# Three token tiles of an expert layer: V rows gathered per pick, or a whole V table multiplied by scattered weights

## The chip, the cores and the metric

The kernel runs on one core of one Trainium2 chip. The metric is device time in microseconds of one execution. The kernel before takes 4022.99 us (median of three runs, 4022.44 to 4024.96).

## The reference, cut to what matters

The reference is one block of an encoder over 1,024 tokens of width 1,024: a combined projection, an SSD mixer, neighbourhood attention, a merge and an output projection with a residual add, and then a layer of many small experts (PEER), a residual add and a last RMS norm. The change touches the expert layer, of which this is the core:

```python
PEER_HEADS = 8; PEER_NKEYS = 128; PEER_EXPERTS = 128 * 128; PEER_TOPK = 16; PEER_CHUNK = 128
def chunk(xc):                                   # 128 tokens
    q = (xc @ w_q).reshape(PEER_CHUNK, PEER_HEADS, 2, PEER_DHALF)
    s = jnp.einsum('thzd,znd->thzn', q, sub_keys).astype(jnp.float32)
    s1, i1 = lax.top_k(s[:, :, 0], PEER_TOPK)
    s2, i2 = lax.top_k(s[:, :, 1], PEER_TOPK)
    ...                                          # the 16 best pairs of each head: top, eidx
    gate = jax.nn.softmax(top, axis=-1)
    act = jax.nn.gelu(jnp.einsum('thkd,td->thk', u[eidx], xc).astype(jnp.float32), approximate=False)
    return jnp.einsum('thk,thkd->td', (gate * act).astype(v.dtype), v[eidx])
# then h = h + g2 * peer(n2), out = rms_norm(h, final_g)
```

Each token picks 8 x 16 = 128 experts. Tables u and v have 16,384 rows of 1,024 f32 (4 KB a row, 67.1 MB a table). The output of a token is the sum of its 128 picked v rows, each with its weight (gate times GELU of the dot product of the token with the picked u row).

## The kernel before

The kernel is written engine by engine, with semaphores. A front half (`stage_condition`, `stage_front`, `stage_ssd`) makes the projections and part of the SSD mixer. `stage_tail` does the rest. Its time is divided into slots. A tile has 128 tokens, and there are 8 tiles (TT = 8). Slot n = 128 i + j belongs to pick j of tile i, and each engine goes through all slots in order and does in a slot what is listed for it there:

- POOL issues the gather of U rows for pick j (L2459): an indirect DMA that brings, for each of the 128 tokens, the u row that it picked, 128 rows of 4 KB into one of RU = 6 places of a ring. It first waits until the place was used (`u_used`).
- DVE forms the 128 dot products of a U gather with the tokens' rows, which lie in PSUM (L2637), and from slot to slot also the routing (top 16, best pairs) of the tile that comes next.
- A grain is two heads, 32 picks. When its dot products are done, ACT takes GELU (L2489) and DVE multiplies by the gates (`weigh`, L2586). PE transposes the grain's indices and weights (`turn_index`, `turn_weight`), and ACT spreads the weights into a matrix (L2500).
- POOL gathers the V rows of the grain (L2452): 32 indirect DMAs, each with 32 picks of four tokens, into one of RV = 12 places. A V gather comes 45 slots behind its pick, one in a slot. PE multiplies every four of them by the spread weights and adds them up in PSUM (`add_experts`, L2683); after the fourth grain of a tile, DVE adds the residual and norms, and SP stores the tile.
- Between these, in the same slots, run the "lane" jobs: for the six later tiles gates, late SSD, attention, merge, output projection and query scores (L1775 are the products of 128x128 weights with 512 columns, f32). They are placed in slots by a cost table, pass by pass, so that the tiles 2p and 2p+1 are ready 12 slots before slot 256 p. The last lane job lies ahead of tile 6: tiles 6 and 7 have none.

So in every slot POOL issues one U gather and, from slot 45 on, one V gather: 1,024 of each, 512 KB each. All loads and stores that are not indirect go through SP's one queue, in program order.

In `stage_front`, SP first loads the blocks w_x of the x projection and copies weights for later from one place in memory to another (`kept_scr`, L487); then it goes through `items`, the gate projections: eight blocks n of 512 columns, each times 8 or 2 token tiles. For block n+1 it loads two halves of w_z (`load_z`, L465) and stores each result (`v_scr`, `zg_scr`, L505) from one of four staging places:

```python
for m, (n, t) in enumerate(items):
    if n + 1 < CB and t in (0, 1):
        sp.wait_ge(z_lo, n * KD + (t + 1) * KH)
        load_z(2 * (n + 1) + t)
```

Of the kernel before, what the change touches and what calls it, by code (L numbers as in the profile page):

```python
# [19 lines left out]
P = 128  # L20
SEQ, DM = 1024, 1024
# [27 lines left out]
LATE_BLOCKS = 6 + 2 + 2 + QW // HALF  # L49


def build_program(nc, a, out):
# [20 lines left out]
    mask_scr = scratch("mask_scr", [P, 4, P])  # L73
    late_ssd = (x_scr, state_scr, bc_scr, tab_scr, mask_scr)
# [3 lines left out]
    with top:  # L78
# [29 lines left out]
        with mid:  # L108
# [12 lines left out]
            with front:  # L121
# [8 lines left out]
                stage_front(nc, a, opener, banks, sem, w_in, ident, ones, n1, cT, X, BT, CT, dt, dA, rpb_scr, zg_scr, v_scr, qk_scr, mod_scr, rpm_scr, kept_scr,  # L130
# [4 lines left out]
        stage_tail(nc, a, opener, banks, sem, ident, mod_scr, rpm_scr, n1_scr, qk_scr, zg_scr, v_scr, y_scr, h_scr, w_scr, kept_scr, w_in,  # L135
# [213 lines left out]
def stage_front(nc, a, opener, banks, sem, w_in, ident, ones, n1, cT, X, BT, CT, dt, dA, rpb_scr, zg_scr, v_scr, qk_scr, mod_scr, rpm_scr, kept_scr, ahead, ps_x0, x_order, split_room, rows_kept):  # L349
# [22 lines left out]
    with ctx:  # L372
# [22 lines left out]
        with ExitStack() as room:  # L395
# [11 lines left out]
            b_ada = sb("b_adaB", [MB, P])  # L407

# [20 lines left out]
        s_kept_w = sem("b_keptw")  # L429
        s_bias, s_kept = [sem("q_bias0"), sem("q_bias1")], [sem("q_kept0"), sem("q_kept1")]  # L430
# [25 lines left out]
        with nc.Block() as block:  # L456
            @block.sync
            def _(sp):
# [29 lines left out]

                for m, (n, t) in enumerate(items):
# [33 lines left out]
                sp.wait_ge(s_kept_w, 16 * LATE_BLOCKS)  # L523

            @block.gpsimd
            def _(pool):
                nc.gpsimd.memset(padded[:, :, 0:2], 0.0).then_inc(edge_done, 1)
# [646 lines left out]
def stage_tail(nc, a, opener, banks, sem, ident, mod_scr, rpm_scr, n1_scr, qk_scr, zg_scr, v_scr, y_scr, h_scr, w_scr, kept_scr, w_in, y_rstd, late_ssd, y_kept, out, s_out):  # L1174
# [14 lines left out]
    with ctx:  # L1189
# [8 lines left out]
        h = n2  # L1198
        qs = sb("qs", [P, 2, QW])
        small = qs[:, 1, :]  # L1200
        ring = sb("ring", [P, (RU + RV) * DM])
        u_rows = ring[:, 0:RU * DM].rearrange("p (r d) -> p r d", d=DM)
        v_rows = ring[:, RU * DM:].rearrange("p (r d) -> p r d", d=DM)
# [21 lines left out]
        idx_f = sb("idx_f", [P, RI, PICKS])  # L1225
# [3 lines left out]
        weight = sb("weight", [P, PICKS])  # L1229
# [12 lines left out]
        lstat = sb("lstat", [P, 4])  # L1242
        nmax = sb("nmax", [P, 2])
        rsum = sb("rsum", [P, 4])
        rinv = sb("rinv", [P, 4])
        ystat = sb("ystat", [P, 2])
# [38 lines left out]
            sem("f_accread"), sem("f_fmean"), sem("f_froot"), sem("f_fin"), sem("f_chain"))  # L1285

# [945 lines left out]
        with nc.Block() as block:  # L2232
# [26 lines left out]
            def _(pool):  # L2259
                nc.gpsimd.iota(iota_i[:, :], pattern=[[1, TOPK]], base=0, channel_multiplier=0).then_inc(iota_done, 1)  # L2260
                nc.gpsimd.memset(spread[:, :, :], 0.0).then_inc(zero_done, 1)
# [461 lines left out]
```

## Time and profile before

| | |
|---|---|
| median of three runs | 4022.99 us (4022.44 to 4024.96) |
| span of the profiled execution | 4023.9 us, from the first to the last instruction |
| PE, DVE, POOL, ACT busy | 69%, 61%, 53%, 21% of the span |
| moved by DMA | 1,423 MB, 354 GB/s over the span |
| of it by POOL's queue (indirect DMAs and a few more) | 1,086.75 MB |
| of it by SP's queue | 332.95 MB |

The three runs lie on both sides of the span of the profiled execution. POOL's busy time holds the generation of its DMAs, not their transfer. The front half ends at about 900 us, where the first U gather is issued; the slots of `stage_tail` fill the rest. L2474 copies the normalized rows of a tile into PSUM at the tile's first slot, when the last dot product of the tile before is done; its eight starts, 897.7, 1283.3, 1706.4, 2102.9, 2517.6, 2885.9, 3287.9 and 3620.4 us, cut the tail into tiles.

### The profile page before, as it was taken

What the parts mean: (1) busy time and instruction counts of PE and PEld (TensorE: products, weight loads), DVE (VectorE), ACT (ScalarE), POOL (GpSimd) and SP (SyncE); (2) the same over time, 40 slices, a digit from 0 to 9 for tenths busy, and PEclk for the clock granted to TensorE, in tenths of its full rate; (3) what the DMA queues carried; (4) which work ended last, traced back from release to release, by engine and by line L of the source; (5) the groups of instructions that cost most, each with busy time, mean ns of one, the idle gap of its engine ahead of it and who ended that gap; (6) DMA issues with size and microseconds to landing.
All of it is one profiled execution on the core that took longest, in us unless ns stands there. A gap on an engine that the chain in (4) does not pass through costs nothing.

```text
span 4023.9 us, 41489 instructions
## 1 busy us (share of the span) xinstructions
PE 2788.8 (69%) x14155; PEld 1429.4 (36%) x14155; DVE 2439.3 (61%) x5186; ACT 858.2 (21%) x2057; POOL 2121.6 (53%) x2149
## 2 busy tenths in 40 slices
PE   6899999898975677796676767455757753333334
PEld 4787777544342322333333323122323320000000
DVE  4552446527676666556766665677766667666652
ACT  4333213402143301112333011132320110000000
POOL 1000205013576656556766565676665667777775
PEclk9999999999987888897887888778888875565566
DMA  8944865567999999999999999999999999999998
GB/s 223 258 154 143 228 209 169 180 240 268 413 407 393 403 410 412 413 412 393 393 400 405 412 400 413 401 406 397 392 406 411 389 409 409 410 408 408 402 409 336
DMA packets 472416, 1422.97 MB, mean 354 GB/s; under 512 B 66152, under 2 KB 136784, under 8 KB 464016
## 3 DMA queue, kind: packets, MB, share of 16 engines
q0 software_dynamic: 298768, 1086.75, 69.5%
q1 hardware_dynamic: 173152, 332.95, 23.2%
q8 instruction: 115, 1.88, 0.2%
q10 hardware_dynamic: 288, 0.62, 0.1%
q14 instruction: 93, 0.76, 0.0%
HBM read 1359.46 MB, written 90.06 MB: 360 GB/s over the span
## 4 chain that ended last, share of the span: by engine, by line
DMA 38%; POOL 13%; PE 9%; issue 8%; DVE 8%; ACT 0%; SPq 0%; DVEq 0%; ACTq 0%; POOLq 0%
DMA ring<-in_peer_u,idx 34%; POOL ring L2459 6%; POOL ring L2452 6%; PE ps_l L1775 5%; DMA ring<-in_peer_v,idxT 4%; DVE ring L2637 4%; PE acc L2683 2%; PE ps_l L1853 1%; PE ps_l L1831 0%; DMA lane<-state_scr 0%; DVE e_f L2560 0%; PE ps_l L1848 0%; DVE hit L2558 0%; DVE where L2520 0%; DVE rest L2521 0%
## 5 line engine op out<-in xcount | busy, mean ns | idle before, releaser
L2637 DVE CUSTOM_DVE_ANT_0 ring<-ring,ps_n2F 128x1024 f32<-128x1024 f32 x1024 | 1242.2, 1220 | 933.3 <-DMA ring<-in_peer_u,idx 922.2
L2459 POOL DMA_INDIRECT ring<-in_peer_u,idx x1024 | 999.1, 976 | 805.8 <-DVE dots L2637 576.3
L2683 PE MATMUL acc<-ring,spread 128*32 128x512 f32 x4096 | 734.7, 853 | 953.3 <-DMA ring<-in_peer_v,idxT 953.1
L2452 POOL DMA_INDIRECT ring<-in_peer_v,idxT x1024 | 993.0, 970 | 336.5 <-issue 297.5
L1775 PE MATMUL ps_l<-lane 128*128 128x512 f32 x1760 | 790.2, 603 | 11.6 <-ACT lane L2100 6.6
L2683 PEld LDWEIGHTS acc<-ring,spread 128*32 128x32 f32 x4096 | 147.7, 136 | 1417.6 <-issue 1415.7
L1775 PEld LDWEIGHTS ps_l<-lane 128*128 128x128 f32 x1760 | 330.8, 193 | 443.8 <-issue 431.4
L562 POOL DMA_DIRECT2D bias<-rpb_scr x16 | 13.2, 829 | 322.5 <-PE ps_dt L846 277.0
L1970 PE MATMUL ps_l<-lane 128*128 128x512 f32 x192 | 117.3, 696 | 56.1 <-DVE nmax L2152 55.8
L2489 ACT ACTIVATE dots<-dots 128x32 f32<-128x32 f32 x32 | 7.3, 229 | 606.1 <-DVE dots L2637 605.9
L2060 ACT ACTIVATE st<-st,nmax 128x512 f32<-128x512 f32 x128 | 92.2, 720 | 184.0 <-DVE nmax L2152 182.9
L846 PE MATMUL ps_x<-n_hi,w_x_hi 128*128 128x512 f32 x256 | 103.9, 406 | 13.1 <-DVE w_x_lo L681 13.1
L846 PE MATMUL ps_x<-n_hi,w_qk_hi 128*128 128x512 f32 x256 | 103.2, 403 | 6.6 <-DVE w_qk_lo L757 6.6
L688 DVE TENSOR_TENSOR w_z_lo<-w_z,w_z_hi 128x512 fp32r<-128x512 f32 x64 | 40.7, 688 | 109.1 <-ACT w_z_hi L588 75.1
L1996 PEld LDWEIGHTS ps_l<-lane 128*64 128x64 f32 (+1 forms) x1664 | 66.2, 146 | 108.0 <-ACT lane L2040 56.5
L846 PE MATMUL ps_x<-n_lo,w_x_hi 128*128 128x512 f32 x256 | 102.3, 399 | 0.0
L846 PE MATMUL ps_x<-n_hi,w_x_lo 128*128 128x512 f32 x256 | 102.1, 399 | 0.0
L846 PE MATMUL ps_x<-n_lo,w_qk_hi 128*128 128x512 f32 x256 | 101.9, 398 | 0.0
L846 PE MATMUL ps_x<-n_hi,w_qk_lo 128*128 128x512 f32 x256 | 101.8, 397 | 0.0
L1996 PE MATMUL ps_l<-lane 128*64 128x64 f32 (+1 forms) x1664 | 84.4, 241 | 23.2 <-ACT lane L2040 22.9
L2018 PE MATMUL ps_l<-ident,st 128*128 128x128 f32 x448 | 73.9, 289 | 31.5 <-ACT lane L2049 31.1
L2266 POOL TENSOR_TENSOR ring<-lane,ring 128x4096 f32<-128x4096 f32 x2 | 17.7, 8832 | 139.7 <-DMA lane<-in_w_out 139.7
(363 smaller groups left out, 4014.7 us busy)
## 6 DMA issues: line engine op xcount, KB each, us to landing
lane<-kept_scr SPq DMA_DIRECT2D x44, 2048.0 KB, 10.6
w_z<-in_w_in SPq DMA_DIRECT2D x16, 1024.0 KB, 6.0
adaB<-in_w_ada SPq DMA_DIRECT2D x16, 1024.0 KB, 6.2
ring<-in_peer_u,idx POOLq DMA_INDIRECT x1024
ring<-in_peer_v,idxT POOLq DMA_INDIRECT x1024, 13.8
kept_scr<-in_w_in SPq DMA_DIRECT2D x6, 2048.0 KB
lane<-w_scr SPq DMA_DIRECT2D x6, 2048.0 KB, 10.9
ada<-in_w_ada SPq DMA_DIRECT2D x8, 1024.0 KB, 15.4
```

What stands on the lines that cost most here:

```text
L688: nc.vector.tensor_tensor(z_parts[1][q % PLACES][:, :], w_z[:, k // KH, k % KH, :], z_parts[0][q % PLACES][:, :], ALU.subtract).then_inc(z ...
L846: last = nc.tensor.matmul(bank, stationary(left, k), moving(right, k), start=(k == 0 and n == 0), stop=(k == KD - 1 and n == 2))
L1775: last = nc.tensor.matmul(bank, inT[:, f % SETS, k, :], spare_half(c, k // 4)[:, k % 4, :] if weights is None else weights[:, k, :], start ...
L1853: last = nc.tensor.matmul(ps_y[:, h * HEADDIM:(h + 1) * HEADDIM], M4[:, d, h, :], x_dt[:, i, d, hc], start=False, stop=(d == 1 and h == HP ...
L1970: nc.tensor.matmul(scores_bank(a_pass, u), qd[:, p % RP, i, :], kT[:, p % RP, k0:k0 + HALF], start=True, stop=True).then_inc(qk_done, 1)
L1996: last = nc.tensor.matmul(values_bank(a_pass, u)[side(hh), :], PT[keys, u % 2, b, side(hh)], V[keys, p % RP, tile, side(hh)], start=(j == ...
L2018: last = nc.tensor.transpose(turned[:, b * P:(b + 1) * P], probs[:, u % RS, c0:c0 + P], ident[:, :])
L2060: nc.scalar.activation(row[:, GRID_W:], row[:, GRID_W:], ACT.Exp, bias=least, scale=-1.0, accum_out=rsum[:, u % 4:u % 4 + 1]).then_inc(exp ...
L2452: pool.indirect_dma_start(v_rows[:, nv % RV, :], None, a["peer_v"][0], bass.IndirectOffsetOnAxis(ap=idxT[:, m % 2, col:col + 1], axis=0)). ...
L2459: pool.indirect_dma_start(u_rows[:, n % RU, :], None, a["peer_u"][0], bass.IndirectOffsetOnAxis(ap=idx[:, i % RI, j:j + 1], axis=0)).then_ ...
L2637: nc.vector.tensor_tensor_reduce(out=u_rows[:, n % RU, :], in0=u_rows[:, n % RU, :], in1=ps_n[:, :], scale=1.0, scalar=0.0, op0=ALU.mult, ...
L2683: last = nc.tensor.matmul(acc[q * QUAD:(q + 1) * QUAD, cols], spread[:, m % 2, c0:c0 + QUAD], v_rows[:, nv % RV, cols], start=(g == 0 and ...
```

## The change

For tiles 2, 3 and 4 the V rows are no longer gathered. For each of these tiles there is a matrix in memory (`share_scr`, 16,384 experts by 128 tokens, f32, 8.4 MB), filled with zeros in `stage_front` by three DMAs on SP's queue, in pieces of 1 KB, between the loads of w_x and `items`. When a grain of such a tile is weighed, DVE works out for each pick the place of (expert, token) in the matrix (`share_cells`), and POOL issues for each pick an indirect DMA that adds 128 weights, one for each token, to 128 words there. These scatters come 40 slots behind the start of their grain, 16 in 10 slots and then 6 slots of none, and each 16 (a head) wait until all before them of the tile have landed.

From six slots ahead of tile 6 until 18 slots behind tile 7's last U gather, SP streams the whole V table in 32 shares of 4 x 128 rows (2 MB) with the matching parts of the three matrices (3 x 256 KB), two shares in flight. PE multiplies: 6 units for each share (3 tiles x 2 halves of the columns), each of 4 products of 128x128 by 512, one PSUM bank of the lane's three; DVE adds each unit to a sum in SBUF. Then the three tiles get their residual, norm and store.

The V gathers of tiles 0 and 1 are spread over the slots of tiles 0 to 4, 2.5 slots apart (`pace`); those of tiles 5 to 7 stay 45 slots behind their picks. The V ring has 10 places in place of 12, and the residual row h gets a place of its own there (it was n2's).

```diff
+DENSE = (2, 3, 4)
+KEYS_TOGETHER = 4
+SHARES = NKEYS // KEYS_TOGETHER
+SHARE_FILL = 256
...
+                sp.wait_ge(nothing_done, 1)
+                for scr in share_scr:
+                    rows = scr.rearrange("(p r n) o -> p r (n o)", p=P, n=SHARE_FILL)
+                    sp.dma_start(rows, nothing[:, :].unsqueeze(1).broadcast_to([P, NKEYS * NKEYS // SHARE_FILL, SHARE_FILL])).then_inc(s_filled, 16)
 
                 for m, (n, t) in enumerate(items):
...
-    RU, RV, RI = 6, 12, 2
+    RU, RV, RI, RH = 6, 10, 2, 4
...
-        GELU_AT, WEIGHT_AT, TURN_W_AT, SPREAD_AT = 0, 3, 4, 6
-        TURN_I_AT, IDXT_AT = 14, 20
-        FETCH_AT, SUM_AT = 13, 16
+        GELU_AT, WEIGHT_AT = 0, 3
+        TURN_I_AT, IDXT_AT, TURN_W_AT, SPREAD_AT = -31, -25, -9, -7
+        FETCH_AT = 45
+        SHARE_AT, SHARE_PACE = 40, 10
...
+        SUMMED = [t for t in range(TT) if t not in DENSE]
+        BEFORE = [t for t in SUMMED if t < DENSE[0]]
+        v_grain = [GRAINS * t + g for t in SUMMED for g in range(GRAINS)]
+        pace = GRAINS * (DENSE[-1] + 1) / (GRAINS * len(BEFORE))
+
+        def fetch_slot(s, k):
+            m = v_grain[s]
+            if m < GRAINS * DENSE[0]:
+                return FETCH_AT + int(pace * (s * GRAIN + k))
+            return m * GRAIN + FETCH_AT + k
...
+                share_at.setdefault(m * GRAIN + SHARE_AT + k // TOPK * TOPK + k % TOPK * SHARE_PACE // TOPK, []).append((t, j))
...
+        DENSE_FROM, DENSE_TO, DENSE_LAG = PICKS * 6 - 6, PICKS * TT + 18, 2
+        unit_slot = [DENSE_FROM + q * (DENSE_TO - DENSE_FROM) // ALL_BLOCK_UNITS for q in range(ALL_BLOCK_UNITS)]
...
+        def load_shares(sp, c):
+            if c == 0:
+                sp.wait_ge(p_mm, LANE_JOBS)
+                sp.wait_ge(p_norm, TT)
+                for r in range(MIX):
+                    sp.wait_ge(s_keep[r], 16 * TT // MIX)
+            if c >= 2:
+                sp.wait_ge(block_mm, (c - 1) * UNITS_A_SHARE)
+            sp.dma_start(v_block[:, c % 2, :, :], v_blocks[c]).then_inc(s_block[c % 2], 16)
+            for i in range(ND):
+                if c == 0:
+                    sp.wait_ge(s_share[i], 16 * PICKS)
+                sp.dma_start(shares[:, c % 2, i, :], share_scr[i].rearrange("(c b n) o -> c b (n o)", b=NKEYS, n=KEYS_TOGETHER * P)[c]).then_inc(s_part[c % 2], 16)
...
+                        for t, pick in share_at.get(n, ()):
+                            d, g = DENSE.index(t), pick // GRAIN
+                            if pick % GRAIN == 0:
+                                pool.wait_ge(weight_done, GRAINS * t + g + 1)
+                                pool.wait_ge(cell_done, GRAINS * d + g + 1)
+                            if pick and pick % TOPK == 0:
+                                pool.wait_ge(s_share[d], 16 * pick)
+                            pool.indirect_dma_start(share_scr[d], bass.IndirectOffsetOnAxis(ap=cell[:, g % 2, pick % GRAIN:pick % GRAIN + 1], axis=0),
+                                                    weight[:, t % RH, pick:pick + 1], None, compute_op=ALU.add).then_inc(s_share[d], 16)
...
+                def add_block(q):
+                    c, i, half = block_unit(q)
+                    total = whole[i][:, half * HALF:(half + 1) * HALF]
+                    bank = ps_l[:, q % LANE_BANKS * HALF:(q % LANE_BANKS + 1) * HALF]
...
+                    v.wait_ge(block_mm, q + 1)
+                    if c == 0:
+                        nc.vector.tensor_copy(total, bank).then_inc(block_added, 1)
+                    else:
+                        v.wait_ge(block_added, q - UNITS_A_SHARE + 1)
+                        nc.vector.tensor_tensor(total, total, bank, ALU.add).then_inc(block_added, 1)
...
+                def multiply_block(q):
+                    c, i, half = block_unit(q)
+                    bank = ps_l[:, q % LANE_BANKS * HALF:(q % LANE_BANKS + 1) * HALF]
...
+                    if q % UNITS_A_SHARE == 0:
+                        pe.wait_ge(s_block[c % 2], 16 * (c // 2 + 1))
+                        pe.wait_ge(s_part[c % 2], 16 * ND * (c // 2 + 1))
+                    if q >= LANE_BANKS:
+                        pe.wait_ge(block_added, q - LANE_BANKS + 1)
+                    for k in range(KEYS_TOGETHER):
+                        last = nc.tensor.matmul(bank, shares[:, c % 2, i, k * P:(k + 1) * P], v_block[:, c % 2, k, half * HALF:(half + 1) * HALF],
+                                                start=(k == 0), stop=(k == KEYS_TOGETHER - 1))
+                    last.then_inc(block_mm, 1)
```

## Rows read from the trace of the kernel before

**Rows 1.** The page's slices: the span in 40 equal parts.

```profile
DMA  8944865567999999999999999999999999999998
GB/s 223 258 154 143 228 209 169 180 240 268 413 407 393 403 410 412 413 412 393 393 400 405 412 400 413 401 406 397 392 406 411 389 409 409 410 408 408 402 409 336
```

**Rows 2.** Busy time by tile: length; PE, PEld, DVE, ACT, POOL (instructions); clock, DMA, GB/s.

```profile
897.70:1283.30 385.60, 307.54 (x1309) 150.81 (x1310) 273.30 (x643) 107.52 (x282) 221.63 (x222) 0.89 0.94 366
1283.30:1706.40 423.10, 310.24 (x1752) 136.78 (x1750) 261.71 (x614) 86.96 (x232) 246.81 (x256) 0.88 1.03 409
1706.40:2102.90 396.50, 291.03 (x1500) 133.90 (x1498) 262.84 (x602) 113.10 (x311) 258.53 (x257) 0.86 1.02 399
2102.90:2517.60 414.70, 301.51 (x1525) 128.80 (x1526) 257.15 (x590) 73.78 (x188) 246.97 (x256) 0.83 1.02 407
2517.60:2885.90 368.30, 212.08 (x1280) 94.91 (x1279) 262.79 (x602) 100.33 (x287) 252.16 (x258) 0.79 1.03 400
2885.90:3287.90 402.00, 284.94 (x1476) 119.91 (x1474) 256.25 (x590) 71.34 (x182) 244.50 (x255) 0.84 1.01 402
3287.90:3620.40 332.50, 116.83 (x576) 25.23 (x576) 228.25 (x519) 20.24 (x49) 244.73 (x256) 0.56 1.03 409
3620.40:4023.90 403.50, 154.14 (x776) 33.26 (x776) 216.61 (x461) 23.02 (x55) 276.74 (x292) 0.58 0.98 389
```

**Rows 3.** The page's costliest groups: the two gathers on POOL.

```profile
L2459 POOL DMA_INDIRECT ring<-in_peer_u,idx x1024 | 999.1, 976 | 805.8 <-DVE dots L2637 576.3
...
L2452 POOL DMA_INDIRECT ring<-in_peer_v,idxT x1024 | 993.0, 970 | 336.5 <-issue 297.5
```

**Rows 4.** POOL's timeline in tile 0: start, length, instruction, idle before.

```profile
1037.76 0.94 POOL L2452 DMA_INDIRECT ring<-in_peer_v,idxT  x1 [0.30 <-issue]
1039.00 0.95 POOL L2459 DMA_INDIRECT ring<-in_peer_u,idx  x1 [0.30 <-issue]
```

**Rows 5.** POOL's waits, tiles 2 to 4, then 6 and 7: us, times, longest.

```profile
POOL ring L2459 <- DVE dots L2637: 243.5, 185, 7.0
...
POOL ring L2459 <- DVE dots L2637: 35.0, 45, 1.9
```

**Rows 6.** Busy time of L1775 alone in tile 0: length; PE, PEld; clock.

```profile
897.70:1283.30 385.60, 170.03 (x384) 73.10 (x384) 0.89 0.94 366
```

**Rows 7.** Busy time of L2683 alone in tiles 0, 1 and 6.

```profile
897.70:1283.30 385.60, 45.73 (x320) 9.60 (x320) 0.89 0.94 366
1283.30:1706.40 423.10, 79.65 (x512) 16.82 (x512) 0.88 1.03 409
...
3287.90:3620.40 332.50, 115.96 (x512) 21.77 (x512) 0.56 1.03 409
```

**Rows 8.** POOL's issues: a direct one's group, and the V gather's shortest, median, longest.

```profile
L572 POOL DMA_DIRECT2D rpm_scr<-bias x8 | 4.7, 587 | 2.4 <-POOL bias L569 2.4
...
L2452 POOL DMA_INDIRECT ring<-in_peer_v,idxT x1024: 939/945/1996, 1016.6 to 4003.8; - x171
```

**Rows 9.** POOL's queue from 60 to 100 us: packets, MB, share of 16 engines.

```profile
q0 software_dynamic: 589, 1.87, 55.7%
```

**Rows 10.** The page's DMA issues: the V gather, median us to landing.

```profile
ring<-in_peer_v,idxT POOLq DMA_INDIRECT x1024, 13.8
```

**Rows 11.** Busy time in 640 to 660 us, where SSD states are written out.

```profile
640.00:660.00 20.00, 20.00 (x75) 13.91 (x74) 16.50 (x15) 15.86 (x50) 15.62 (x7) 1.00 0.89 320
```

**Rows 12.** DVE's groups: adding a PSUM bank to 512 columns.

```profile
L2213 DVE TENSOR_TENSOR lane<-lane,ps_l 128x512 f32<-128x512 f32 x14 | 9.6, 685 | 19.2 <-PE ps_l L1775 19.2
```

**Rows 13.** The front: 232 to 262 us in 40 slices; then SP's timeline.

```profile
GB/s 22 0 79 115 320 382 399 415 412 377 344 344 322 358 344 347 336 341 382 377 188 107 3 0 0 0 0 0 0 0 0 0 0 0 0 0 0 0 0 22
...
267.60 0.37 SPq L465 DMA_DIRECT2D w_z<-in_w_in  x1
...
281.10 33.96 SPq L505 DMA_DIRECT2D v_scr<-staged  x7
...
320.30 0.36 SPq L505 DMA_DIRECT2D v_scr<-staged  x1
```

More of the change, by code:

```diff
@@ L407, in stage_front @@
             b_ada = sb("b_adaB", [MB, P])
+            nothing = sb("nothing", [P, SHARE_FILL])
         ps_x = [ps_x0, banks(ctx, "ps_x1", 2)]
@@ new lines, in stage_tail @@
+        fetch_at, sum_at, turn_i_at, idxT_at, turn_w_at, spread_at = {}, {}, {}, {}, {}, {}
+        for s in range(len(v_grain)):
+            for k in range(GRAIN):
+                fetch_at.setdefault(fetch_slot(s, k), []).append((s, k))
+            for b in range(BATCHES):
+                sum_at.setdefault(fetch_slot(s, b * QUADS + QUADS - 1), []).append((s, b))
+            for at, after in ((turn_i_at, TURN_I_AT), (idxT_at, IDXT_AT), (turn_w_at, TURN_W_AT), (spread_at, SPREAD_AT)):
+                at[fetch_slot(s, 0) + after] = s
@@ new lines, in stage_tail @@
+        ended_at = {t: fetch_slot(GRAINS * (order[t] + 1) - 1, GRAIN - 1) for t in SUMMED}
+        fin_at, square_at, root_at, norm_at, out_at, back_at = (
+            {ended_at[t] + after: t for t in SUMMED} for after in (FIN_AT, SQUARE_AT, ROOT_AT, NORM_AT, OUT_AT, BACK_AT))
+        share_at = {}
+        for t in DENSE:
+            for j in range(PICKS):
+                m, k = GRAINS * t + j // GRAIN, j % GRAIN
+                share_at.setdefault(m * GRAIN + SHARE_AT + k // TOPK * TOPK + k % TOPK * SHARE_PACE // TOPK, []).append((t, j))
@@ new lines, in stage_tail @@
+        for c in range(SHARES):
+            block_at.setdefault(unit_slot[(c - 1) * UNITS_A_SHARE] + 1 if c >= 2 else DENSE_FROM - 6 + c, []).append(c)
+        WHOLE_SUM = DENSE_TO + DENSE_LAG + 2
+        RESIDUAL_SLOT, WHOLE_ROOT, WHOLE_NORM = PICKS * (TT - 1) + 8, WHOLE_SUM + 3 * ND + 1, WHOLE_SUM + 3 * ND + 4
+        LANE_JOBS = len(evac_of)
+        LANE_ACTS, LANE_DVES = acts, dves
+        DROOM = KEYS_TOGETHER * DM
+        v_block = lane[:, 0:2 * DROOM].rearrange("p (r a d) -> p r a d", r=2, a=KEYS_TOGETHER)
@@ L2440, in _ @@
                         n = i * PICKS + j
-                        m, k = fetched(n)
-                        if m is not None:
+                        for m, k in fetch_at.get(n, ()):
                             nv = m * GRAIN + k
@@ L2638, in _ @@
                                                            op0=ALU.mult, op1=ALU.add, accum_out=dots[:, j:j + 1]).then_inc(u_used, 1)
+                        for q in added_at.get(n, ()):
+                            add_block(q)
+                        if 0 <= n - WHOLE_SUM < 3 * ND and (n - WHOLE_SUM) % 3 == 0:
+                            whole_sum((n - WHOLE_SUM) // 3)
+                        if n == WHOLE_SUM + 3 * ND:
+                            v.wait_ge(whole_sq, ND)
+                            nc.vector.tensor_scalar(lstat[:, 0:ND], lstat[:, 0:ND], 1.0 / DM, EPS, ALU.mult, ALU.add).then_inc(whole_mean, 1)
+                        if 0 <= n - WHOLE_NORM < ND:
+                            i_d = n - WHOLE_NORM
+                            if i_d == 0:
+                                v.wait_ge(whole_root, 1)
+                                link(nc.vector.reciprocal(lstat[:, 0:ND], lstat[:, 0:ND]))
+                            nc.vector.scalar_tensor_tensor(out=residual[i_d], in0=residual[i_d], scalar=lstat[:, i_d:i_d + 1], in1=final_g[:, :],
+                                                           op0=ALU.mult, op1=ALU.mult).then_inc(whole_done, 1)
                         for job in job_at.get(n, ()):
```

230 lines of the change are left out of this document (150 added, 80 removed).

## The prediction

> **What bounds the kernel now.** I read the slices of the page first, then the busy time of the engines stretch by stretch, cut at the eight copies of a tile's normalized rows into PSUM (L2474, first at 897.7 us). The slices show two kernels in one: up to about 900 us a front half in which the DMA engines have gaps, and behind it some 3,100 us in which they are full at about 400 GB/s [rows 1]. The table by tile says the same in numbers: in tiles 1 to 6 the DMA share is 1.01 to 1.03 at 399 to 409 GB/s, while PE is busy for 35 to 73% and DVE for 62 to 71% [rows 2]. Tile 6 carries nothing but its 256 gathers of 512 KB: 332.5 / 256 = 1.30 us for one [rows 2].
>
> The reader is to see that POOL is nearly as full. One gather holds it for 0.97 us on the mean [rows 3] and 0.30 us of issue stands between two that wait for nothing, so that two of the shortest follow each other every 1.25 us [rows 4]. I use 0.97 + 0.30 = 1.27 us. Two in a slot are 2.54 us, in a slot of tile 6 that takes 2.60. The waits bear it out: in tiles 2 to 4 POOL waited 243.5 us for DVE to give a U row back (DVE itself waits for rows to land), in tiles 6 and 7 only 35.0 us [rows 5]. So the stage has two limits, 1.30 us of DMA for a gather and 1.27 us of POOL for any indirect DMA, whatever it moves. The change treats them differently.
>
> **The change, part by part.** POOL: 384 V gathers go (3 tiles of 128) and 384 scatter-adds come, one for each pick, so POOL still issues 2,048 indirect DMAs. DMA: 384 x 1.30 = 499 us go; 67.1 MB of V table and 25.2 MB of matrices come. What counts is where.
>
> *Tiles 0 to 5.* The V gathers of tiles 0 and 1 now come at 0.4 a slot from slot 45 to 682: 34 in tile 0 (before 83), 51 in each of tiles 1 to 4 (before 128), 18 in tile 5, with 83 of tile 5's own (101, before 128). The scatters come from slot 296 to 672, 16 to a head: 93 in tile 2, 128 in each of tiles 3 and 4, 35 in tile 5. For each tile I take the later of what is left of the DMA time and POOL's count at 1.27:
> - tile 0: 49 gathers fewer are 64 us of DMA. But PE was busy 308 of 386 us, 170 of them in the products of L1775 [rows 2, 6], and loses only 49 x 4 records x 0.14 = 28 us [rows 7]. I take the middle, -46.
> - tile 1: 77 fewer are -100, which leaves 323; DVE and PE were busy 262 and 310 us in it [rows 2], in bursts, so I take 335: -88.
> - tile 2: DMA 397 - 100 = 297; POOL (128 + 51 + 93) x 1.27 = 345: -51.
> - tile 3: DMA 315; POOL 307 x 1.27 = 390: -25.
> - tile 4: DMA 268; POOL 390 against 368 before: +22.
> - tile 5: 27 fewer, -35; POOL 264 x 1.27 = 335 is below the 367 that stay.
>
> Sum: -223. The trace has no scatter, so its two costs are bounded. On POOL, below, by the cheapest issue of a DMA there, 0.59 us for 128 rows of 4 KB (L572); above, by the longest gather, 2.00 us [rows 8]. I take the gather's 0.97: the same kind of instruction with one offset for each of 128 partitions. On the DMA engines, below nothing; above by the bias rows, written to memory in runs of 256 bytes: 1.87 MB took 55.7% of 16 engines for 40 us, so 7,300 runs at 49 ns [rows 9]. 128 words are 8 for each engine, 0.39 us, and twice that, 0.78, if each add also reads. At most that is 100 us in a tile, and POOL's surplus over DMA (48, 75 and 122 us in tiles 2 to 4) covers it but for 25 us in each of tiles 2 and 3. I take 0.4 us, hidden. Sixteen scatters wait for the sixteen before them. Behind the wait stand U and V gathers in POOL's queue, but seven slots of 1.4 gathers, 12 us, lie between, and a V gather lands in 13.8 us in a full queue [rows 10], which POOL's pace empties: nothing. The index arithmetic on DVE is some six operations on 32 elements for each of 12 grains: nothing, under waits for U rows.
>
> A rule speaks against the scatters: the Trainium skill (DMA: Bandwidth & Descriptors, Rules for kernel authors) says that transfers under 64 KB are mostly overhead, and one scatter moves 512 bytes. By that page's fixed 2.0 us of one DMA, an estimate if they ran one by one is 768 us; the trace agrees that cost does not go by bytes on POOL [rows 3, 8], but shows issues overlapping with data.
>
> *Tiles 6 and 7.* From slot 762 to 1042 SP streams 32 shares of 2 MB of V and 768 KB of matrices: 92.3 MB at tile 6's full 409 GB/s are 226 us, and these tiles have no free DMA time [rows 2]: +226.
>
> For that rate the Trainium skill (DMA: Bandwidth & Descriptors, Specifications) gives a memory limit of about 358 GB/s for one core; by it the stream would cost 258 us, an estimate. The 409 GB/s of this trace decides.
>
> PE gets 768 products of 128x128 by 512. One is two records (512 records for 128 gathers, two products each [rows 7]) of 0.443 us [rows 6]: 1,536 x 0.443 = 680 us. The 301 V gathers left there are 1,204 records x 0.156 = 188 [rows 7]. 868 us of 736 + 226 = 962: covered, if the granted clock comes up from 0.56 as PE fills; it was 1.00 where PE was busy throughout [rows 11] and 0.88 at 73% [rows 2]. Four records of acc behind a late gather hold up the products behind them, so I add 20. DVE's 192 additions at 0.69 us [rows 12] are 132 us over the 445 that it was busy, of 962: nothing. The three dense tiles are finished before tile 7's last gathers: nothing.
>
> *Front.* Three fills of 8.4 MB enter SP's queue behind the last copies of weights, which drain at about 249 us, and ahead of the second block's w_z load (267.6 us) and the v_scr stores [rows 13]. Writes went at 320 GB/s with a share of 0.89 [rows 11], so 360 full: 25.2 MB take 70 us, to 319. The w_z half lands 4 us later, and the split of a slice takes 1.5. The second block's first result was stored at 320.3 us, and one takes 5.6 (the seven before it came from 281.1 on) [rows 13], so PE began it near 314; now it waits until near 325: +11 (nothing at 410 GB/s or if the loads overtake; +40 at 250).
>
> Sum: 4023.9 + 11 - 223 + 226 + 20 = 4058. The span is 0.9 us above the median of the runs, so 4057, 0.8% slower.
>
> **The rivals.**
> 1. *The scatter is cheap on POOL.* At 0.59 us its cadence is 0.89. Tile 2 falls to (179 x 1.27 + 93 x 0.89) = 310, tiles 3 and 4 to 341: 35 + 49 + 49 = 133 less, 3924, faster; with 0.4 us of DMA for each, DMA holds them at 334, 366 and 341, and it is 3973. For it: direct issues of as many rows cost 0.59 [rows 8]. Against: all 2,048 indirect ones cost 0.94 or more. It decides from about 0.85 us.
> 2. *The scatter is dear.* An add may need a read descriptor more for each word. At 1.4 us, halfway to the bound, 384 x 0.43 = 165 more: 4222; at 2.00, 4453. On the DMA side a read of memory for each word ends at 0.78 us, 50 us more: 4107. The Trainium skill (DMA: Bandwidth & Descriptors, Specifications) says that below 512 bytes the DMA engines read, modify and write; no row here shows it.
> 3. *PE bounds the end.* If the clock stayed at 0.57, a record would take 0.78 us and 1,536 of them 1,190; with acc (1,204 x 0.226) 1,470 against 962: 4545. Against: rows at full use show 1.00. A mild form, with 60 us of waits between PE, DVE and blocks in place of the 20, gives 4097.
> 4. *The fills and the pace cost nothing.* No front stall, no PE waits, and tiles 0 and 1 at their DMA limit (-64, -100): 4057 - 11 - 20 - 30 = 3996, faster.
>
> **How the numbers follow.** The forecast of about 4057 has 0.45; rival 1 0.17; rival 2 0.20, a third of it near 4107; rival 3 0.10, mostly its mild form; rival 4 0.08. 0.2% (8 us) is about what a measurement of this kernel can tell from no change. Faster is rivals 1 and 4: 0.25. Within 0.2%, 4015 to 4031, is an edge of the forecast's own spread of 45 us either way (scatters at 0.12 us less or more on POOL): 0.05. Slower is the rest, 0.70. The range goes from rival 1 to rival 2's middle, 3920 to 4240; outside lie the dear scatter's far end and PE at the low clock, together 0.15.
>
> **What would show it.** Right: POOL 90% busy or more in tiles 3 and 4 with gaps in the DMA share there; tiles 0 and 1 shorter, tile 4 not; the time from tile 6 to the end longer by 220 to 260 us with DMA full; PE waiting near 320 us in the front. Wrong: scatters far from 0.97 us on POOL, or a full DMA share in tiles 3 and 4 (then the words cost the engines more than 0.8 us), or PE full at a low clock at the end.

## The result, and the profile after

The changed kernel takes 4399.09 us in the median of four runs (4393.75 to 4404.06), the kernel before 4023.14 in the same comparison: 1.0931 times as long, with an interval of 1.0914 to 1.0949. That is 376 us more; 34 were forecast, in a range that ends at 4240. The direction was right, the size and the range were not. The profiled execution has a span of 4402.3 us.

The page's slices after the change, the span in 40 parts of 110 us, beside [rows 1]:

```profile
POOL 1000313125455557888888788887755555555553
PEclk9999999999879998767787756777789999999998
DMA  8995865579899999778888777777999999999997
GB/s 211 271 326 179 231 186 162 188 300 371 300 355 388 410 413 327 198 222 254 270 274 289 240 223 200 225 231 227 366 409 410 408 408 408 407 407 407 399 408 263
```

Before, DMA was full from 900 us to the end. Now there is a valley of about 1,400 us in its middle, at 200 to 290 GB/s, and POOL stands at its highest exactly there. The busy time by tile, with the columns of [rows 2], shows where the valley lies:

```profile
912.90:1270.50 357.60, 289.56 (x1094) 151.03 (x1094) 271.52 (x641) 106.99 (x279) 170.70 (x169) 0.88 0.87 326
1270.50:1597.80 327.30, 263.53 (x1402) 127.38 (x1401) 253.24 (x604) 82.42 (x218) 173.58 (x178) 0.91 1.01 394
1597.80:2030.60 432.80, 268.53 (x1161) 136.12 (x1159) 263.76 (x618) 111.22 (x302) 325.42 (x269) 0.78 0.84 271
2030.60:2509.70 479.10, 270.98 (x1166) 125.85 (x1166) 252.84 (x605) 69.36 (x173) 381.65 (x308) 0.74 0.83 265
2509.70:2990.10 480.40, 180.88 (x933) 93.83 (x934) 260.96 (x616) 95.79 (x277) 386.54 (x308) 0.66 0.75 219
2990.10:3419.40 429.30, 296.92 (x1393) 127.86 (x1392) 258.08 (x599) 70.58 (x178) 284.57 (x273) 0.82 0.96 362
3419.40:3859.30 439.90, 385.57 (x1276) 149.44 (x1274) 281.52 (x607) 20.12 (x48) 243.88 (x256) 0.94 1.03 408
3859.30:4402.30 543.00, 463.13 (x1576) 175.97 (x1576) 295.09 (x580) 23.28 (x56) 274.36 (x290) 0.92 0.96 376
```

Against [rows 2] the front ends 15 us later (tile 0 begins at 912.9, before at 897.7). Tiles 0 and 1 are 28 and 96 us shorter. Tiles 6 and 7 are 247 us longer together, forecast were 246. The miss is all in tiles 2 to 5: they were to become 89 us shorter and became 240 us longer. In tiles 3 and 4 POOL's busy time and 0.30 us behind each of its 308 instructions make 382 + 92 = 474 and 387 + 92 = 479 us, nearly the whole of 479 and 480. The page's costliest groups say which instruction it is, to be read against [rows 3]:

```profile
L2555 POOL DMA_INDIRECT ring<-in_peer_u,idx x1024 | 1003.3, 980 | 859.4 <-DVE dots L2792 617.2
...
L2548 POOL DMA_INDIRECT ring<-in_peer_v,idxT x640 | 616.9, 964 | 284.8 <-issue 185.7
L2869 PE MATMUL ps_l<-lane 128*128 128x512 f32 x1536 | 692.3, 606 | 9.4 <-DMA lane<-share_scr_t 9.4
L2564 POOL DMA_INDIRECT share_scr_t<-ring,cell x384 | 620.5, 1616 | 118.0 <-issue 117.1
```

Both gathers cost what they cost before. The scatter-add (L2564) holds POOL for 1.62 us, not 0.97. POOL's timeline in tile 3 shows that nothing else stands between (start, length, instruction, idle before):

```profile
2204.24 1.00 POOL L2548 DMA_INDIRECT ring<-in_peer_v,idxT  x1 [0.30 <-issue]
2205.54 0.97 POOL L2555 DMA_INDIRECT ring<-in_peer_u,idx  x1 [0.30 <-issue]
2206.81 1.61 POOL L2564 DMA_INDIRECT share_scr_t<-ring,cell  x1 [0.30 <-issue]
2208.73 1.57 POOL L2564 DMA_INDIRECT share_scr_t<-ring,cell  x1 [0.31 <-issue]
```

And POOL's waits from 1700 to 3050 us, the whole stretch of the scatters but its two ends (us in all, times, longest), beside [rows 5], where POOL had waited 243.5 us for DVE in tiles 2 to 4:

```profile
POOL share_scr_t L2564 <- issue: 111.0, 363, 0.7
POOL ring L2555 <- issue: 95.1, 312, 0.3
POOL ring L2548 <- issue: 43.0, 141, 0.3
POOL ring L2555 <- DVE dots L2792: 17.2, 44, 2.9
```

The slack of 243.5 us is down to 17. A scatter takes 1.62 + 0.30 = 1.92 us of POOL, so 384 of them take 0.65 x 384 = 249 us more than forecast. That is not all of it: tiles 2 to 5 missed by 329.

### The profile page after: what moved, and what is told of

Same layout as the page of the kernel before. It is cut to its first block, busy times and chain, and to the rows that moved or that the text cites. A ratio compares the mean times of both kernels' runs of the same rounds, so it can differ in the third digit from the quotient of the medians.

```text
span 4402.3 us, 41387 instructions
## 1 busy us (share of the span) xinstructions
PE 3232.1 (73%) x13963; PEld 1694.1 (38%) x13963; DVE 2556.2 (58%) x5434; ACT 841.1 (19%) x2003; POOL 2371.1 (54%) x2151
## 4 chain that ended last, share of the span: by engine, by line
DMA 26%; POOL 21%; PE 10%; issue 9%; DVE 6%; ACT 1%; POOLq 0%; DVEq 0%; ACTq 0%
DMA ring<-in_peer_u,idx 19%; POOL share_scr_t L2564 11%; POOL ring L2555 7%; DMA ring<-in_peer_v,idxT 7%; POOL ring L2548 3%; PE ps_l L1795 3%; PE ps_l L2869 3%; DVE ring L2792 2%; PE acc L2852 2%; PE ps_l L2016 0%; PE ps_l L1990 0%; DVE e_f L2666 0%; DVE hit L2664 0%; PE ps_l L2038 0%; DVE hit L2656 0%
## 5 line engine op out<-in xcount | busy, mean ns | idle before, releaser
L2852 PE MATMUL acc<-ring,spread 128*32 128x512 f32 x2560 | 417.5, 783 | 665.8 <-DMA ring<-in_peer_v,idxT 665.7
L1795 PE MATMUL ps_l<-lane 128*128 128x512 f32 x1760 | 789.2, 605 | 27.1 <-ACT st L2125 9.4
L2548 POOL DMA_INDIRECT ring<-in_peer_v,idxT x640 | 616.9, 964 | 284.8 <-issue 185.7
L2869 PE MATMUL ps_l<-lane 128*128 128x512 f32 x1536 | 692.3, 606 | 9.4 <-DMA lane<-share_scr_t 9.4
L2564 POOL DMA_INDIRECT share_scr_t<-ring,cell x384 | 620.5, 1616 | 118.0 <-issue 117.1
L1795 PEld LDWEIGHTS ps_l<-lane 128*128 128x128 f32 x1760 | 334.8, 194 | 461.5 <-issue 440.3
L2869 PEld LDWEIGHTS ps_l<-lane 128*128 128x128 f32 x1536 | 290.8, 194 | 410.8 <-issue 393.5
L2852 PEld LDWEIGHTS acc<-ring,spread 128*32 128x32 f32 x2560 | 85.6, 129 | 928.3 <-issue 927.7
L1990 PE MATMUL ps_l<-lane 128*128 128x512 f32 x192 | 138.9, 814 | 136.9 <-DVE columns L2172 136.9
L2080 ACT ACTIVATE st<-st,columns 128x512 f32<-128x512 f32 x128 | 92.2, 721 | 225.0 <-DVE columns L2172 223.9
L2016 PE MATMUL ps_l<-lane 128*64 128x64 f32 (+1 forms) x1664 | 94.3, 261 | 31.5 <-ACT lane L2060 31.5
L2734 DVE TENSOR_TENSOR st<-st,ps_l 128x512 f32<-128x512 f32 x124 | 84.8, 684 | 49.2 <-PE ps_l L2869 46.8
```

The costliest lines, as they stand in the source:

```text
L1795: last = nc.tensor.matmul(bank, inT[:, f % SETS, k, :], spare_half(c, k // 4)[:, k % 4, :] if weights is None else weights[:, k, :], start ...
L1990: nc.tensor.matmul(scores_bank(a_pass, u), qd[:, p % RP, i, :], kT[:, p % RP, k0:k0 + HALF], start=True, stop=True).then_inc(qk_done, 1)
L2016: last = nc.tensor.matmul(values_bank(a_pass, u)[side(hh), :], PT[keys, u % 2, b, side(hh)], V[keys, p % RP, tile, side(hh)], start=(j == ...
L2080: nc.scalar.activation(row[:, GRID_W:], row[:, GRID_W:], ACT.Exp, bias=least, scale=-1.0, accum_out=rsum[:, u % 4:u % 4 + 1]).then_inc(exp ...
L2548: pool.indirect_dma_start(v_rows[:, nv % RV, :], None, a["peer_v"][0], bass.IndirectOffsetOnAxis(ap=idxT[:, m % 2, col:col + 1], axis=0)). ...
L2564: pool.indirect_dma_start(share_scr[d], bass.IndirectOffsetOnAxis(ap=cell[:, g % 2, pick % GRAIN:pick % GRAIN + 1], axis=0), weight[:, t % ...
```

## The experiments

The theory had two parts. First, POOL's own time for a scatter-add sets the pace of tiles 2 to 4. Second, my sum took the later of two limits for a whole tile, where the kernel passes through stretches with different limits one after the other. The rivals: the scatters' words hold up memory or the DMA engines; the granted clock, 0.66 to 0.78 in tiles 2 to 4, makes PE the bound; the stream or the fills are the price. Each experiment is one run with a profile; the kernel before took 4022.47 to 4025.88 us beside them.

**No scatter.** The other waits on the scatters' semaphores, on SP and DVE, go with it.

```diff
-                            if pick and pick % TOPK == 0:
-                                pool.wait_ge(s_share[d], 16 * pick)
-                            pool.indirect_dma_start(share_scr[d], bass.IndirectOffsetOnAxis(ap=cell[:, g % 2, pick % GRAIN:pick % GRAIN + 1], axis=0),
-                                                    weight[:, t % RH, pick:pick + 1], None, compute_op=ALU.add).then_inc(s_share[d], 16)
```

> The 384 scatter-adds and the waits on them are left out; the matrices stay zero, so the experts of tiles 2 to 4 add nothing. Theory: in tiles 2 to 5 POOL's own time per scatter (1.62 us busy and 0.30 of issue) sets the pace, so up to 384 x 1.92 = 737 us of POOL go, tiles 2 to 4 fall to what DMA or PE leaves (300 to 330 us each, from 433, 479 and 480), tile 5 to about 375: 3860 to 3930 us in all. Rival, that the tiles are long because PE runs at a clock of 0.66 to 0.74 there: they stay above 400 us and the total stays above 4200.

Measured: 3901.69 us. Busy time of tiles 2 to 5 without scatters, the columns as above:

```profile
1593.50:1923.00 329.50, 249.55 (x1159) 128.76 (x1159) 261.21 (x618) 110.70 (x303) 181.28 (x182) 0.86 0.95 363
1923.00:2249.50 326.50, 248.74 (x1172) 117.52 (x1174) 250.54 (x605) 68.83 (x174) 172.75 (x179) 0.86 0.98 386
2249.50:2535.80 286.30, 161.83 (x934) 86.80 (x934) 255.97 (x616) 95.22 (x277) 180.95 (x181) 0.76 0.99 368
2535.80:2915.80 380.00, 278.37 (x1394) 121.93 (x1393) 256.81 (x599) 70.22 (x178) 227.29 (x232) 0.87 1.02 404
```

In tiles 2 to 4 the same PE work now fits into 286 to 330 us, at a higher clock, though nothing on PE was changed; so PE was not the bound, and the low clock went with PE's waiting. The valley in the DMA share is gone (0.95 to 1.02). The scatters cost 4399 - 3902 = 497 us in all. Without them the change would be faster than the kernel before by 121 us, so a scatter was allowed to cost 121 / 384 = 0.32 us. The last row is the first sign for the theory's second part: tile 5 holds 35 scatters and took 429, without them 380, though POOL is busy for only 227 of the 380 us.

**The scatter without the add.**

```diff
-                                                    weight[:, t % RH, pick:pick + 1], None, compute_op=ALU.add).then_inc(s_share[d], 16)
+                                                    weight[:, t % RH, pick:pick + 1], None).then_inc(s_share[d], 16)
```

> The same scatters without the add: a word that two heads pick keeps the later weight. Theory that the add makes the scatter dear on POOL: the instruction falls from 1.62 to about 0.97 us, as a gather, and the total by up to 384 x 0.65 = 249 us to about 4150. Rival, that writing to 128 places in memory costs 1.6 us with or without an add: 4399 as before. Rival, that reads for the add hold up the DMA engines: the instruction stays at 1.6 us, the tiles get shorter all the same.

**A gather of words in its place.** `words` is a spare stretch of 32 columns behind the weights.

```diff
-                            pool.indirect_dma_start(share_scr[d], bass.IndirectOffsetOnAxis(ap=cell[:, g % 2, pick % GRAIN:pick % GRAIN + 1], axis=0),
-                                                    weight[:, t % RH, pick:pick + 1], None, compute_op=ALU.add).then_inc(s_share[d], 16)
+                            pool.indirect_dma_start(words[:, pick % GRAIN:pick % GRAIN + 1], None, share_scr[d],
+                                                    bass.IndirectOffsetOnAxis(ap=cell[:, g % 2, pick % GRAIN:pick % GRAIN + 1], axis=0)).then_inc(s_share[d], 16)
```

> In place of each scatter-add a gather of one word for each partition from the same 128 cells into a spare column: the matrices stay zero. If the direction (memory as the target) is what costs, it holds POOL for 0.94 to 1.0 us like the gathers of 4 KB rows, and the total is 4150. If the size of 4 bytes is what costs, it holds POOL for about 1.6 us and the total is about 4399.

**Half of the words, and an eighth.** The second is the same edit with `P // 8`.

```diff
-                            pool.indirect_dma_start(share_scr[d], bass.IndirectOffsetOnAxis(ap=cell[:, g % 2, pick % GRAIN:pick % GRAIN + 1], axis=0),
-                                                    weight[:, t % RH, pick:pick + 1], None, compute_op=ALU.add).then_inc(s_share[d], 16)
+                            pool.indirect_dma_start(share_scr[d], bass.IndirectOffsetOnAxis(ap=cell[0:P // 2, g % 2, pick % GRAIN:pick % GRAIN + 1], axis=0),
+                                                    weight[0:P // 2, t % RH, pick:pick + 1], None, compute_op=ALU.add).then_inc(s_share[d], 16)
```

> Each scatter-add takes only the first 64 partitions, so 64 words in place of 128; the other 64 tokens of tiles 2 to 4 get no experts. If POOL works through the descriptors one by one, the instruction takes about half, 0.8 us, and the total falls by 384 x 0.8 = 311 us to 4090, less what other limits take over. If the price is a fixed one for each instruction, 1.6 us and 4399.

> Each scatter-add takes only the first 16 partitions, 16 words in place of 128 (the other 112 tokens of tiles 2 to 4 get no experts). From 128 words (1.58 us in the median) to 64 (1.44) the instruction lost 2.2 ns a word; if the rest is a price for each add instruction, it holds POOL for about 1.34 us and the total is 384 x 0.24 = 92 us below 4399, about 4305. Rival, that 64 words hit a floor or a step: 1.44 and 4355.

Measured: 4187.54 without the add, 4164.74 with word gathers, 4354.76 with 64 words, 4306.66 with 16. The groups of POOL in these four kernels, one fence each in that order (busy us, mean ns of one, idle before):

```profile
L2564 POOL DMA_INDIRECT share_scr_t<-ring,cell x384 | 394.5, 1027 | 118.8 <-issue 116.4 <-DVE cell L2717 1.8 <-DVE dots L2792 0.6
```

```profile
L2565 POOL DMA_INDIRECT ring<-share_scr_t,cell x384 | 378.7, 986 | 118.8 <-issue 116.2 <-DVE cell L2718 1.7 <-DVE dots L2793 0.9
```

```profile
L2564 POOL DMA_INDIRECT share_scr_t<-ring,cell x384 | 574.4, 1496 | 118.0 <-issue 117.0 <-DVE cell L2717 0.9
```

```profile
L2564 POOL DMA_INDIRECT share_scr_t<-ring,cell x384 | 523.9, 1364 | 117.7 <-issue 116.4 <-DVE cell L2717 1.0 <-DVE dots L2792 0.3
```

It is the add. The target in memory costs next to nothing (1.03 us against 0.99 for a gather of the same words), the size neither (0.99 for 4 bytes, 0.98 for 4 KB). The add costs 1.62 - 1.03 = 0.59 us more, and about half of that or more is a price of the instruction: from 128 words to 16 it falls by only 0.25 us, 2.25 ns a word, which makes some 0.29 us for all 128. The idea that POOL works off 128 descriptors one by one at half the price for half of them fell with the run of 64 words.

The Trainium skill (Collectives: The Full Stack, the paragraph on why ReduceScatter is half of AllGather) says that an add in the DMA engines takes two source reads and so two read descriptors where a copy takes one. By that rule alone the extra should go with the number of words; the rows show an add of 16 words that still takes 1.36 us, more than a plain scatter of 128. What makes up that fixed part no run here shows.

The second thing to see is that 4164.74 is not 4057. With word gathers POOL's price was 0.986 us, the one I had put into the sum, the cells and the waits were the same, and still the sum missed by 108. So the price was one of two errors.

**The V stream.**

```diff
-            sp.dma_start(v_block[:, c % 2, :, :], v_blocks[c]).then_inc(s_block[c % 2], 16)
+            if c < 2:
+                sp.dma_start(v_block[:, c % 2, :, :], v_blocks[c]).then_inc(s_block[c % 2], 16)
...
-                        pe.wait_ge(s_block[c % 2], 16 * (c // 2 + 1))
+                        pe.wait_ge(s_block[c % 2], 16)
```

> Only the first two of the 32 shares of V are loaded (4.2 of 67.1 MB); the products run over old rows, so the experts of tiles 2 to 4 come out wrong. Theory that DMA bounds the last two tiles (share 1.03 at 408 GB/s): 62.9 MB at 409 GB/s are 154 us, total about 4245. Rival, that the dense products on PE bound them (849 of 983 us busy): the total falls by less than 40 us. POOL's 546 gathers at 1.27 us are 693 us, below both.

Measured: 4261.63, 137 us less, near the 154 of DMA-bound tiles. The last two tiles, with the columns as above and the last one cut at 4046 us:

```profile
3420.70:3784.50 363.80, 361.71 (x1262) 142.49 (x1262) 280.60 (x606) 20.13 (x49) 241.85 (x253) 1.00 1.03 406
3784.50:4046.00 261.50, 261.50 (x905) 103.22 (x907) 197.62 (x428) 16.30 (x37) 175.80 (x183) 1.00 1.02 403
```

Here PE is busy nearly throughout at the granted clock of 1.00, over both tiles for 808 of 839 us: with the stream gone, PE is as near to being the bound as DMA, which fits the 17 us that are missing. With the stream PE was busy for 849 of 983 us, so DMA bounds these tiles but for their end, by a thin margin.

**The fills.** `fill(part)` writes zeros to one of the 48 pieces.

```diff
-                for scr in share_scr:
-                    rows = scr.rearrange("(p r n) o -> p r (n o)", p=P, n=SHARE_FILL)
-                    sp.dma_start(rows, nothing[:, :].unsqueeze(1).broadcast_to([P, NKEYS * NKEYS // SHARE_FILL, SHARE_FILL])).then_inc(s_filled, 16)
...
                     sp.dma_start(dst, src).then_inc(s_st[m % STAGED], 16)
+                    for part in range(m * fills // len(items), (m + 1) * fills // len(items)):
+                        fill(part)
```

> The three zero fills of 8.4 MB are cut into 48 pieces of 0.5 MB, which SP issues one or two at a time between the front's results in place of all together ahead of them. Theory that the 15 us in the front are the wait of the second block's weights behind the fills: most of it comes back, 4384. Rival, that 25.2 MB more take their time on the DMA engines wherever they stand: 4399.

Measured: 4413.99, not the 4384 of the theory; nothing came back. The second block's first store came at 324.38 us (335.74 with the fills together, 320.30 before), so that wait was indeed the fills' place in the queue. But later blocks of the front then came later (the last load of w_z was issued at 435.61 us, with the fills together at 427.25), and tile 0 began at 923.6 in place of 912.9. My theory for the front fell: what was won in one block's weights was lost in the next ones'. That spreading makes the front longer in all is not shown by one run: with the front unchanged, the run without the add began tile 0 at 921.4. With a single fill (the run of one dense tile, below) tile 0 began at 900.1, 2.4 us later than before.

**Other tiles, one tile, and the V gathers early.** These five move the scatters or the gathers beside them. The last two have the edits of the first and the third together, and in the last one the add is taken out as above.

```diff
-DENSE = (2, 3, 4)
+DENSE = (1, 2, 3)
```

> Tiles 1 to 3 in place of 2 to 4 go the dense way: as many scatters, gathers, fills and bytes. 88 scatters fall into tile 1, where POOL was busy for 174 of 327 us, and only 40 into tile 4. Theory that a stretch lasts as long as its own slowest engine: tile 1 372, tiles 2 and 3 449 each ((128 + 32) x 1.27 + 128 x 1.92), tile 4 390, tile 5 400, about 4300 in all. Rival, that the sum over the whole stage counts (POOL's total is the same): 4399.

```diff
-DENSE = (2, 3, 4)
+DENSE = (2,)
```

> Tile 2 alone goes the dense way: 128 scatters, 1,920 gathers, one matrix, the whole V table all the same. Theory that the scatters on POOL are the price: 0.65 us more than a gather for each, in a tile of 439 us ((128 + 85) x 1.27 + 88 x 1.92), and 185 us for 75.5 MB at the end, about 4155: faster than three dense tiles, slower than none. Rival, that the stream at the end is the price and more dense tiles pay it back: 4400 or more, as less is saved for the same 67.1 MB.

Measured: 4373.15 for tiles 1 to 3, 73 us over the expectation, and 4248.02 for tile 2 alone, 93 over. Both are between the theory and its rival, and both misses lie mostly in the tiles in which scatters start or end (tile 1 of the first took 419 us, not 372; tiles 2 and 3 of the second 474 and 443). I had made the prediction's own mistake again and taken tile 1, and tile 3 of the second run, as one piece. The busy time of the changed kernel, cut where the scatters begin in tile 2 and where they have ended in tile 5, shows what a piece is:

```profile
1597.80:1688.00 90.20, 90.12 (x251) 37.86 (x250) 62.01 (x152) 18.88 (x30) 48.91 (x52) 1.00 1.02 413
1688.00:2030.60 342.60, 178.41 (x911) 98.26 (x909) 201.75 (x467) 92.33 (x272) 276.50 (x217) 0.72 0.79 234
...
2990.10:3140.00 149.90, 79.06 (x562) 36.70 (x561) 87.29 (x230) 39.06 (x110) 118.73 (x102) 0.70 0.84 274
3140.00:3419.40 279.40, 217.86 (x832) 91.15 (x831) 170.79 (x370) 31.53 (x68) 165.84 (x172) 0.89 1.02 410
```

Tile 2 begins with 90 us in which PE and the DMA engines are full and POOL has room; then POOL takes over, 276.5 + 217 x 0.30 = 342 of 342.6 us. Tile 5 goes the other way: 118.7 + 102 x 0.30 = 149 of 149.9 us of POOL, then 279 us of DMA at 410 GB/s. The room that POOL has in one piece is of no use in the other. The two rows of tile 3 with one dense tile, cut in the same way, say the same, 172 and 271 us, where a sum over the whole tile at the same prices is (128 + 113) x 1.27 + 40 x 1.92 = 383:

```profile
2106.60:2279.00 172.40, 98.14 (x660) 44.77 (x661) 90.11 (x238) 41.27 (x116) 136.23 (x119) 0.68 0.87 293
2279.00:2549.90 270.90, 202.71 (x793) 84.16 (x792) 167.26 (x359) 31.46 (x67) 161.56 (x167) 0.86 1.02 413
```

The word gathers show it at the price that the sum had. From the first of them in tile 2 to the tile's end, and at the start of tile 5, POOL is full again, 218.9 + 218 x 0.30 = 284 of 286 us and 59.6 + 62 x 0.30 = 78 of 78 us:

```profile
1689.00:1974.70 285.70, 175.23 (x911) 99.42 (x909) 201.87 (x467) 92.50 (x272) 218.94 (x218) 0.76 0.84 281
2771.70:2850.00 78.30, 50.65 (x466) 26.89 (x466) 57.65 (x158) 30.35 (x86) 59.56 (x62) 0.85 0.84 285
```

So the expectations that follow were made by pieces. If they are right, gathers moved out of the scatters' pieces into pieces that DMA bounds shorten the kernel, though 126 gathers more (211 in tiles 0 and 1 in place of 85; the expectation says 124), 164 us of DMA at 1.30, then stand in tiles that DMA fills.

```diff
-        pace = GRAINS * (DENSE[-1] + 1) / (GRAINS * len(BEFORE))
+        pace = 1
```

> The 256 V gathers of tiles 0 and 1 come at one a slot from slot 45 on (as in the kernel before), so all of them issue before the scatters start, in place of 0.4 a slot through the scatters' stretch. Nothing else changes; tiles 0 and 1 get 124 gathers more. Theory that each stretch lasts as long as its own slowest engine: tiles 0 and 1 go back to 385 and 423, tile 2 to 124 + 88 x 3.19 = 405, tiles 3 and 4 to 128 x (1.27 + 1.92) = 408, tile 5 to 124 + 286 = 410; about 4335, faster than 4399. Rival, that spreading fills room in tiles 2 to 4 which is free: then 4399 plus up to 124 x 1.30 = 161, at most 4560.

> Both moves: tiles 1 to 3 dense, tile 0's V gathers at one a slot. Theory by stretches: 385, then 132 + 88 x 3.19 = 413, 408, 408, 134 + 260 = 394, 414, and 983 for the last two: about 4320. Rival: as with tiles 1 to 3 alone, 4373.

> The same and the scatters without the add (a word that two heads pick keeps the later weight), so 1.33 us a scatter on POOL. Theory by stretches: 385, 132 + 88 x (1.27 + 1.33) = 361, 333, 333, 110 + 260 = 370, 414, 983: about 4095, still slower than the kernel before, so the add alone doesn't decide. Rival, that the add was the whole loss: 4023 or less.

Measured: 4365.53 (expected 4335), 4317.69 (4320) and 4116.31 (4095). The first one's tiles 0 to 5 took 392, 422, 423, 413, 414 and 406 us, where 385, 423, 405, 408, 408 and 410 were expected. Its tiles 3 and 4:

```profile
2147.70:2560.30 412.60, 247.86 (x982) 125.40 (x982) 252.19 (x603) 68.31 (x169) 332.86 (x257) 0.78 0.80 243
2560.30:2974.20 413.90, 137.87 (x669) 87.12 (x670) 259.59 (x615) 93.94 (x268) 335.56 (x258) 0.61 0.70 189
```

POOL still sets them (333 + 257 x 0.30 = 410), now with 257 instructions in place of 308. The rival, that the slow pace used room which was free, fell: the kernel got faster by 34 us. That the second came within 2 us of its expectation is in part luck: tile 4, in which the scatters end, took 367 us where 394 were expected, and tiles 0 to 3 took 23 us more than expected. In the last run tile 4 took 345 where 370 were expected. So the sum by pieces is good to some 25 us in such a tile. In the last run, with neither the add's price nor the worse place, the kernel is still at 4116: scatters at 1.30 us of POOL stand in for gathers at 1.27, so POOL gets nothing back. Tiles 1 to 4 became 192 us shorter than in [rows 2], but the last two 249 longer and the front 18. None of these beats the kernel before, and nothing here points to a version that would with scatters issued on POOL.

## Why the prediction was wrong

By its own steps, in the order of the sum (profiled executions: 4058 forecast, 4402.3 measured, 344 to explain):

- *The front*, +11: it was 15.2. The wait that was forecast came: the second block's first store is 15.4 us later. Spreading the fills did not win it back. The changed kernel's SP timeline, beside [rows 13]:

```profile
236.24 54.64 SPq L499 DMA_DIRECT2D share_scr_t<-nothing  x3
290.92 24.04 SPq L472 DMA_DIRECT2D w_z<-in_w_in  x1
...
335.74 0.36 SPq L517 DMA_DIRECT2D v_scr<-staged  x1
```

- *Tiles 0 and 1*, -46 and -88: -28 and -96. Right in sum to 10 us.
- *Tiles 2 to 5*, -51, -25, +22 and -35: +36, +64, +112 and +27, a miss of 329 in all. Here two steps failed.
- **The first that failed**: "I take the gather's 0.97: the same kind of instruction with one offset for each of 128 partitions." As an indirect DMA it is the same kind, and without the add it costs 1.03. With the add it costs 1.62. At 0.65 us each, 384 make 249 of the 329 us. This is a term that was mis-sized. The bounds, 0.59 and 2.00, held it; but I had put 1.4 and more into the tail as "dear", and the reason for dearness that I gave, a read descriptor more for each word, can be about half of it at most, 0.29 of 0.59 us. The rows before could not show the price: all the DMAs in [rows 3, 8] move 512 KB, and none adds.
- **The second**: "For each tile I take the later of what is left of the DMA time and POOL's count at 1.27." That adds up room and load which lie at different times. Tile 2 missed by 87 us, of which its 93 scatters' price is 60; tile 5 by 62, of which 35 scatters are 23; that leaves 27 and 39 us. The word gathers, which ran at the price that I had assumed, miss the sum by 4163.0 - 4058 = 105 us: 86 in tiles 2 to 5 (30 and 39 of it in tiles 2 and 5), the rest in the small steps (+18 in tile 0, -9 in tile 1, +7 in the front, +3 at the end).
- *DMA words*, 0.4 us a scatter, hidden: hidden they were; the 0.4 itself no run shows. The DMA share in tiles 3 and 4 is 0.83 and 0.75, and POOL waits for no transfer. *The wait behind each sixteen scatters* and *the index arithmetic*, nothing: right, the waits show 0.9 us for DVE's cells.
- *Tiles 6 and 7*, +226 and +20: 246.9 measured, DMA full at 408 GB/s in tile 6, the clock up to 0.94, a dense record at 0.451 us (692.3 / 1536) against 0.443. That the sum is right to 1 us is in part luck, for the 20 had no row behind it. The two tiles moved 90.7 MB more than before, 222 us at 408 GB/s; the other 25 lie mostly at the end, where DMA is no longer full:

```profile
4290.00:4330.00 40.00, 40.00 (x140) 15.66 (x132) 12.17 (x21) 2.38 (x6) 11.23 (x12) 0.95 0.80 299
4330.00:4402.30 72.30, 45.35 (x200) 13.89 (x192) 24.35 (x30) 0.41 (x2) 29.34 (x30) 0.82 0.67 247
```

  There the chain that ended last runs through PE from 4288.6 to 4357.3 us, dense products and gathered sums in turn. So PE did bound the end, at the price of the 20 and not of the 60 in rival 3's mild form; its hard form did not come, and the run without the stream shows how near PE stands behind DMA. The hard form was also priced too high: the 0.443 us were measured at a mean clock of 0.89, so at 0.57 a record would take about 0.69 us, not 0.78, and the total would be about 4409, not 4545, an estimate.
- Most signs of being right came: POOL full in tiles 3 and 4 (80% by its busy time, 99% with the 0.30 us of issue) with gaps in the DMA share, tiles 0 and 1 shorter, tile 4 not. So they did not tell the forecast from rival 2. What did was the first sign of being wrong, scatters far from 0.97 us on POOL. *Rival 2* was the case that came, at a price between its two figures. By its rate, 1.62 us gives 4057 + 249 = 4306; the other 93 are the second step's and the small ones'.

The Trainium skill's rule that I weighed (DMA: Bandwidth & Descriptors, Rules for kernel authors: transfers under 64 KB are mostly overhead) pointed the right way. By that page's 2.0 us for one DMA 384 would be 768 us, an estimate; with 1.92 us of POOL each they take 737, and 497 of these show in the end. That 768 and 737 lie close shows nothing: the one prices whole DMAs that run one by one, the other POOL's issue alone.

## What to carry to other kernels

When a transfer is replaced by many small ones, count the issuing engine's time for each beside the bytes saved: by the sum's terms 384 scatters saved 499 - 226 = 273 us of DMA time, and they took 737 of POOL where the gathers had taken 488. An operation that the trace doesn't have, an add in a DMA above all, is to be measured by itself before three tiles are built on it; the nearest row was wrong by two thirds. And two limits are compared piece by piece, cut where the work on either engine starts or stops: a whole tile's totals hid 66 us here in tiles 2 and 5, and misled two of my own expectations in the same way.

## What the runs showed of the hardware

An indirect DMA's time on POOL hardly depends on what it moves: 0.98 us for 128 rows of 4 KB, 0.99 for 128 words, 1.03 for 128 words written to memory. The Trainium skill (Perfetto Trace Analysis, DMA Instruction — SWDGE (GPSIMD)) says that what the profiler reports for such an instruction ends when the last descriptor is written, not when the data have moved; these rows agree. An accumulating scatter takes 1.62 us for 128 words, 1.50 for 64 and 1.36 for 16. A lower granted clock (0.66 to 0.78 in tiles 2 to 4) was a consequence: with the same PE work and POOL out of the way it was 0.76 to 0.86, and 1.00 where PE was busy throughout.
